# Values' projection of the forgetting attention by seven products, with the roles of stationary and moving operand turned

## The reference

```python
def fox_mixer(h, w_in, b_f, q_gain, k_gain, w_out):
    u = h @ w_in                     # 512 x 1024 times 1024 x (3*1024 + 16)
    q, k, v, f_logit = jnp.split(u, [D_MODEL, 2 * D_MODEL, 3 * D_MODEL], axis=-1)
    q = rms_norm(heads(q), q_gain)
    k = rms_norm(heads(k), k_gain)
    v = heads(v)
    ...                              # causal softmax with a forget term, 16 heads of 64
    return o @ w_out
```

## Time and profile before

| | before |
|---|---|
| time, median of 3 runs | 3028.66 us (3025.91 to 3030.33) |
| span of the profiled execution | 3026.6 us |
| PE busy | 2943.9 us (97%), 17897 matmuls |
| DVE busy | 1770.3 us (58%) |
| ACT busy | 703.9 us (23%) |
| POOL busy | 404.4 us (13%) |
| mean granted TensorE clock | 0.990 |
| HBM traffic | 206.8 MB, mean 68 GB/s |

### The profile page before, as it was taken

One profiled execution on the slowest core, in us unless ns is written; L12 is line 12 of the kernel. 1 busy time (PEld: TensorE's weight loads), 2 busy tenths in 40 slices (PEclk: granted clock), 3 DMA queues, 4 the chain that ended last, 5 costly groups with the idle time before them and its releaser, 6 DMA issues.

```text
span 3026.6 us, 42057 instructions
## 1 busy us (share of the span) xinstructions
PE 2943.9 (97%) x17897; PEld 2496.8 (82%) x17897; DVE 1770.3 (58%) x2388; ACT 703.9 (23%) x1250; POOL 404.4 (13%) x390
## 2 busy tenths in 40 slices
PE   8999999999999999989989999999999999999999
PEld 7878888888778888878678878888888867888888
DVE  4475645564467653531566668887555134888853
ACT  1511100035531110002336532212010174112201
POOL 2112210220002220020023401111020021111101
PEclk9999999999999999999999999999999999999999
DMA  4222221322002223121100022223222200222320
GB/s 137 67 73 91 90 84 60 97 80 73 29 29 84 84 84 112 56 81 47 63 1 4 4 93 84 84 84 105 77 69 84 70 1 28 82 86 84 105 68 37
DMA packets 207573, 209.47 MB, mean 69 GB/s; under 512 B 8996, under 2 KB 206332, under 8 KB 207388
## 3 DMA queue, kind: packets, MB, share of 16 engines
q1 hardware_dynamic: 207100, 206.70, 21.4%
q10 hardware_dynamic: 288, 0.10, 0.0%
HBM read 204.65 MB, written 2.10 MB: 68 GB/s over the span
## 4 chain that ended last, share of the span: by engine, by line
PE 91%; DVE 5%; ACT 2%; issue 1%; POOL 0%; ACTq 0%; DMA 0%; DVEq 0%; POOLq 0%
PE pp L272 63%; PE pp L149 9%; PE pp L1269 4%; PE pp L2881 2%; PE pp L2118 1%; PE pp L1403 1%; PE pp L2101 1%; PE pp L2858 1%; PE pp L1750 1%; DVE arena L348 1%; PE pp L2073 1%; PE pp L2914 1%; PE pp L1426 1%; PE pp L2481 1%; DVE rs L856 1%
## 5 line engine op out<-in xcount | busy, mean ns | idle before, releaser
L272 PE MATMUL pp<-arena 128*128 128x256 f32 (+1 forms) x9072 | 1999.3, 383 | 13.6 <-DVE arena L1091 6.5
L272 PEld LDWEIGHTS pp<-arena 128*128 128x128 f32 x9072 | 1721.6, 190 | 289.9 <-DVE arena L1091 7.7
L149 PE MATMUL pp<-arena 128*128 128x264 f32 (+4 forms) x1312 | 294.4, 384 | 1.2 <-DVE arena L830 1.2
L149 PEld LDWEIGHTS pp<-arena 128*128 128x128 f32 (+3 forms) x1312 | 241.6, 185 | 51.2 <-issue 6.2
L360 ACT COPY arena<-pp 128x528 f32<-128x528 f32 (+1 forms) x62 | 36.1, 582 | 656.3 <-PE pp L272 550.0
L865 POOL TENSOR_TENSOR sq<-sq 128x512 f32<-128x512 f32 (+1 forms) x47 | 78.2, 1664 | 720.8 <-ACT sq L843 717.1
L348 DVE TENSOR_TENSOR arena<-arena 128x256 f32<-128x256 f32 (+5 forms) x196 | 166.0, 870 | 6.5 <-POOL arena L2710 2.4
L2636 ACT ACTIVATE arena<-arena,par 128x528 f32<-128x528 f32 x88 | 68.1, 820 | 385.8 <-DVE arena L2667 385.8
L2710 POOL TENSOR_TENSOR arena<-arena 128x528 f32<-128x528 f32 x44 | 72.0, 1637 | 494.5 <-DVE arena L2679 494.5
L380 DVE TENSOR_TENSOR arena<-arena,pp 128x528 f32<-128x528 f32 (+1 forms) x66 | 46.0, 696 | 140.0 <-PE pp L272 138.0
L321 DVE TENSOR_TENSOR arena<-arena 128x1024 f32<-128x1024 f32 (+2 forms) x66 | 122.9, 1862 | 5.3
(11 more groups left out here) (311 smaller groups left out, 2807.5 us busy)
## 6 DMA issues: line engine op xcount, KB each, us to landing
arena<-in_mlp_w_dram SPq DMA_DIRECT2D x64, 1024.0 KB, 5.5
arena<-in_ffn_up_dram SPq DMA_DIRECT2D x44, 1024.0 KB, 5.1
arena<-in_ffn_down_dram SPq DMA_DIRECT2D x16, 1408.0 KB, 7.3
arena<-in_fox_w_in_dram SPq DMA_DIRECT2D x12, 1024.0 KB, 5.3
arena<-in_lru_w_in_dram SPq DMA_DIRECT2D x8, 1024.0 KB, 7.8
arena<-in_lru_w_out_dram SPq DMA_DIRECT2D x4, 1024.0 KB, 5.2
arena<-in_fox_w_out_dram SPq DMA_DIRECT2D x4, 1024.0 KB, 5.1
arena<-in_rw_wk_dram SPq DMA_DIRECT2D x4, 1024.0 KB, 8.1
```

The lines of the kernel that those rows point to most:

```text
L149: mm = pe.matmul(bank[0:m, h, 0:r.shape[1]], slot[0:kp, kk, j * P:j * P + m], r, start=kt == 0, stop=kt == nk - 1)
L272: return pe.matmul(k.pp[seventh(k, name, n, i) % NB][:, j, 0:hw], stationary[i][:, kk, j * P:(j + 1) * P], moving[i][:, kk, :], start=kk = ...
```

## The change

`fox_va` and `fox_vb` become two seven-product calls, `fox_v0` and `fox_v1`, each over one pair of 256-column blocks, with `turned=True`: the input sums are the stationary operand (128 tokens of them), the weight sums the moving one (256 columns). Products and combination are otherwise those of the other calls. The results go unscaled from DVE into `v` (`v_add`), and ACT scales them there in place, 8 pieces of 128x256 for each call (`v_scaled`), after its `keep_first`. The weight sums get a place of their own (`Sv`, in `raw` and `o`): part 0 of `fox_v0`'s stands inside the combine of `fox_qk3`, part 1 behind `keep_roots`; both parts of `fox_v1`'s stand inside the combine of `fox_v0`, ahead of its add of THREE. POOL copies one input difference (128x1024) into `k.h` after its clears, and PE waits for it ahead of `fox_v0`. The first `values` of attention waits for all 16 scalings. The plan now has 14 tiles here, where it had 8; the number of weight units is the same.

```diff
-def product_seven(pe, k, name, X, S, T, hw, ready, summed):
+def product_seven(pe, k, name, X, S, T, hw, ready, summed, turned=False):
...
         def multiply(i, j, kk):
+            if turned:
+                return pe.matmul(k.pp[seventh(k, name, n, i) % NB][:, j, 0:GW], moving[i][:, kk, j * P:(j + 1) * P],
+                                 stationary[i][:, kk, :], start=kk == 0, stop=kk == half - 1)
...
-    plan_tokens(k, "fox_va", w_in, (2 * D, 2 * D + D // 2), spans, ["act", "dve"])
+    plan_seven(k, "fox_v0", w_in, [(2 * D + GW, 2 * D)])
     k.psum.add(f"fox_sum{NQ - 1}", ["act"] * 4)
-    plan_tokens(k, "fox_vb", w_in, (2 * D + D // 2, 3 * D), spans, ["act", "dve"])
+    plan_seven(k, "fox_v1", w_in, [(2 * D + 3 * GW, 2 * D + 2 * GW)])
...
         turn_roots(e, k, "fox_roots", rspans)
-        product_tokens(e, k, "fox_va", lambda kt, a, b: k.h[:, kt, 1 + a:1 + b], lambda kt: None)
+        e.wait_ge(diff_s, 1)
+        product_seven(e, k, "fox_v0", X, Sv, T, hw, lambda i, kk: None, vsum_s[0], turned=True)
         sums(NQ - 1)
-        product_tokens(e, k, "fox_vb", lambda kt, a, b: k.h[:, kt, 1 + a:1 + b], lambda kt: None)
+        product_seven(e, k, "fox_v1", X, Sv, T, hw, lambda i, kk: None, vsum_s[1], turned=True)
...
         def values(f):
             e.wait_ge(pt_s, 3 * (2 * f + 2))
+            if f == 0:
+                e.wait_ge(v_s, 16)
...
-        read_tokens(k, "fox_va", e, "act", v, k.small[:, 50:55])
+        def v_scaled(n):
+            for q, i in (((0, 0), TWO), ((1, 0), FOUR), ((1, 1), None), ((0, 1), THREE)):
+                if i is None:
+                    e.wait_ge(v_raw, n + 1)
+                else:
+                    was_read(e, k, seventh(k, f"fox_v{n}", 0, i))
+                for t in (2 * q[1], 2 * q[1] + 1):
+                    part = v[:, t, v_col(n, q):v_col(n, q) + GW]
+                    e.activation(part, part, ACT.Copy, scale=k.small[:, 50 + t:51 + t]).then_inc(v_s, 1)
+
+        was_read(e, k, seventh(k, f"fox_qk{NQ - 1}", 0, THREE))
+        keep_first(e, k, "fox_v0", 0, tq, hw)
+        v_scaled(0)
         roots(NQ - 1)
-        read_tokens(k, "fox_vb", e, "act", v[:, :, D // 2:D], k.small[:, 50:55])
+        was_read(e, k, seventh(k, "fox_v0", 0, THREE))
+        keep_first(e, k, "fox_v1", 0, tq, hw)
+        v_scaled(1)
...
+        def v_add(n):
+            def add(e, quarter, w, y, op, g):
+                t, c = 2 * quarter[1], v_col(n, quarter)
+                ins = e.tensor_tensor(v[:, t:t + 2, c:c + GW], w, y, op)
+                if g is None:
+                    ins.then_inc(v_raw, 1)
+                else:
+                    freed(k, g, ins)
+            return add
...
         keep_roots(e, k, "fox_roots", rspans)
-        was_read(e, k, k.psum.base["fox_roots"])
-        read_tokens(k, "fox_va", e, "dve", v, k.small[:, 50:55])
+        e.wait_ge(qk_s, 2 * KT)
+        weight_sums(e, k, "fox_v0", 0, Sv, vsum_s[0], 1)
+
+        def next_v(part):
+            def f(e):
+                filled(e, k, seventh(k, "fox_v0", 0, THREE if part else SIX))
+                weight_sums(e, k, "fox_v1", 0, Sv, vsum_s[1], part)
+            return f
+
+        combine(e, k, "fox_v0", 0, tq, uq, hw, v_add(0), middle=next_v(0), late=next_v(1))
         normed(NQ - 1)
-
-        read_tokens(k, "fox_vb", e, "dve", v[:, :, D // 2:D], k.small[:, 50:55])
+        combine(e, k, "fox_v1", 0, tq, uq, hw, v_add(1))
...
+        filled(e, k, k.psum.base["fox_f"])
+        qin_s.wait(e, 1)
+        e.tensor_copy(in_place(X, T, 0, KH, hw), Tq[3]).then_inc(diff_s, 1)
```

More of the change, by code:

```diff
@@ L1348, in stage_fox @@
     Sq = [k.work(at_v + i * KH * GW, KH, GW) for i in range(3)]
+    Sv = [raw[:, 0:2, :].rearrange("p a b -> p (a b)").rearrange("p (t n) -> p t n", t=KH),
+          o[:, 0:2, :].rearrange("p a b -> p (a b)").rearrange("p (t n) -> p t n", t=KH),
+          raw[:, 2:4, :].rearrange("p a b -> p (a b)").rearrange("p (t n) -> p t n", t=KH)]
     Tq = T + [k.work(at_v + 3 * KH * GW, KH, hw)]
@@ L1351, in stage_fox, with v_col @@
     qsum_s, qin_s = [weight_steps(k, 1) for n in range(NQ)], input_steps(k, 4)
+    vsum_s = [weight_steps(k, 1) for n in range(2)]
+    v_raw, v_s, diff_s = (k.sem("fox_" + n) for n in ("v_added", "v_scaled", "difference_kept"))
+    def v_col(n, quarter):
+        return (2 * n + (0 if quarter[0] else 1)) * GW
     osum_s, oin_s = weight_steps(k, 2), input_steps(k, 4)
@@ L1544, in raw_add @@
             return add
+        def v_add(n):
[7 more added lines that the diff above has]
+            return add
         def next_weights(n, part):
             def f(e):
-                filled(e, k, seventh(k, f"fox_qk{n}", 0, THREE if part else SIX))
-                weight_sums(e, k, f"fox_qk{n + 1}", 0, Sq, qsum_s[n + 1], part)
-            return f if n + 1 < NQ else None
+                if n + 1 < NQ:
+                    filled(e, k, seventh(k, f"fox_qk{n}", 0, THREE if part else SIX))
+                    weight_sums(e, k, f"fox_qk{n + 1}", 0, Sq, qsum_s[n + 1], part)
+                elif part == 0:
+                    weight_sums(e, k, "fox_v0", 0, Sv, vsum_s[0], 0)
+            return f
         def normed(n):
```

## The result

| | before | changed |
|---|---|---|
| time, median | 3028.21 us (3025.91 to 3030.33, 4 runs) | 3039.76 us (3036.83 to 3041.07, 4 runs) |
| ratio, 95% interval | | 1.0037 [1.0025, 1.0048] |
| span of the profiled execution | 3026.6 us | 3039.3 us |
| PE busy | 2943.9 us, 17897 matmuls | 2946.0 us, 17865 matmuls |
| mean granted clock | 0.990 | 0.987 |

The forecast was 7.3 slower, 3036.0 us, with a range of 3031.5 to 3039.5: the first median lies 0.3 us above the range, the second one (3037.07) inside.

A forecast was written before the change was run, and what follows sets the result against it. PE was taken as the bound, 91% of the span. Terms -6.7 + 3.9 + 6.9 - 0.2 + 4.2 - 0.8 gave +7.3 us, 3036.0 from the median 3028.66, range 3031.5 to 3039.5.

The forecast's parts named there:

- the clock: Behind the two new idle stretches around v0 and v1, matmuls run at 1.2 GHz: +4.2 us, bounds 3.0 and 5.9.
- rivals 2 and 4: 2: stalls come, clock holds, +3.1, 3031.8, chance 0.11; 4: one of two clock falls missed, +5.2, 3033.9, chance 0.10.
- Matmuls, -6.7: On PE, fox_va and fox_vb (55.50 us) give way to two calls of 24.41 us: -6.7 us.
- Start of v0, +3.9: Ahead of v0, PE takes ONE and TWO at once, so waits for the next logarithm too: +3.9 us.
- Inside v0, nothing: SIX's weight sums from DVE are ready 0.4 us early, and THREE's delayed add is covered too: nothing.
- Between v0 and v1, +6.9: Sums wait 0.9 us for THREE's add; v1 idles 6.0 for ACT, whose scalings precede the roots: +6.9 us.
- End of v1, -0.2: At v1's end, the last add is one instruction of 0.69 us where two took 0.88: -0.2 us.
- fox_out, -0.8: Six more tiles make start_early true, so fox_out's 0.89 us wait for the last output copy goes: -0.8 us.
- POOL's copy, nothing: POOL's copy behind its clears takes 0.9 to 2.3 us, needed by PE 100 us later: nothing.
- tiles free in time (1): Both calls start where the sums end, without idle stretches or lower clock: -6.8 us, 3021.9; chance 0.07.
- rival 3: Clock falls at every gap, a third at the wait for THREE, each 3.0 us: +12.1, 3040.8; chance 0.10.

The follow-up runs named there:

- the second set: The changed kernel, unaltered, run again seven times beside other kernels: median 3037.07 us against 3028.63 before, ratio 1.0027.
- the dummies' run: Changed kernel plus 9 dummy matmuls in each of fox_v0 and fox_v1 between taking ONE's tile and TWO's: 3030.61 us, ratio 1.0006 of before.
- ONE before TWO: Changed kernel with fox_v0 and fox_v1 running all of ONE before taking TWO's tile: 3032.71 us, ratio 1.0012 of the kernel before.
- the pairs: ACT's roots as two logarithms, then two exponentials: on the moved-weight-sums version 3017.50 us (0.9963), again 3018.62 (0.9966); on the kernel before, plain values, 3023.41 (0.9985).
- the moved weight sums: Changed kernel with ONE before TWO, v0's scaling behind roots(3), and both calls' part 1 weight sums moved: 3021.54 us, ratio 0.9978 of before.
- the one with `fox_out` held back: Changed kernel with start_early forced false, so fox_out doesn't start early: run once, 3038.91 us.
- the one with ACT's scaling moved: Changed kernel with ACT's scaling of v0 moved behind roots(3) and the copy of v1's ONE: 3032.21 us, ratio 1.0013 of before.

## Why the prediction was right

The mechanism came as forecast, term by term, and one term was too small: the clock, 4.2 us where 5.9 were lost. That put the traced cost at the upper bound of the sum (6.1 to 9.0 us without its extra half microsecond) and the first median just outside the range. How near the number came has some luck in it as well. The first set's executions were all of the slower kind, with the lower mean clock; three of the seven in the second set, at 3032.4 to 3034.4 us, lie near rivals 2 and 4 instead.

*Matmuls, -6.7.* Right. At full clock the turned calls are 24.39 us, as the dummies' run shows, and the others 24.41.

*Start of v0, +3.9.* Right in place and size: the wait is 5.73 us instead of 1.79, on the third logarithm.

*Inside v0, nothing.* Right for the changed kernel; SIX has no wait. That the cover was thin was shown when PE started earlier: 2.31 us of wait (the prediction named 0.4 us of cover).

*Between v0 and v1, +6.9.* Measured 0.92 + 5.84 = 6.8. The scalings took 0.91 us a pair in SBUF where I took 0.81 from reads out of PSUM.

*End of v1, -0.2, and fox_out, -0.8.* Measured 1.16 against 1.28 of idle, and 0.89 gone.

*Clock, +4.2.* The mechanism was right and the size too small: 27.43 + 27.25 - 2 x 24.41 = 5.9 us, at the upper bound of 5.9. The mean of four rows drew in two shorter stretches (1.5 and 1.7), where both new gaps were as costly as the dearest row; the second set of runs gave 27.35 and 27.21, so it is no chance of one execution, though three of eleven may have escaped it, as said above. The dummies, which leave PE no long idle stretch ahead of the calls, turn the loss off. The Trainium skill (TensorE: Matmul & The Clock Gate, What's actually happening) puts the ramp's penalty under 1% of a typical span and advises against fitting a count of slow matmuls. 5.9 us are 0.2% of this span and agree with that; but of a change worth some 10 us they are more than half, so that leaving them out would have given rival 2's 3031.8. The Trainium skill also has idle leading to the lower level there, and these traces agree: 0.50 behind both long waits.

*POOL's copy, nothing.* Right. It took 1.03 us beside two DVE adds that read PSUM and kept their 0.68 and 0.69, and the idle behind them kept its 1.60 us. The timeline of POOL:

```profile
623.69 1.03 POOL L1682 COPY arena<-arena 128x1024 f32<-128x1024 f32 x1
```

and of DVE beside it:

```profile
623.22 0.68 DVE L380 TENSOR_TENSOR arena<-sq,pp 128x512 f32<-128x512 f32 x1
623.93 0.69 DVE L383 TENSOR_TENSOR arena<-arena,pp 128x512 f32<-128x512 f32 x1
...
626.94 0.69 DVE L1565 TENSOR_TENSOR arena<-arena,pp 128x512 f32<-128x512 f32 x1 [1.60 <-PE pp L275]
```

Summed up, the part between `fox_qk3` and `fox_out` is 9.1 us by the trace (10.04 to the scores, 0.9 back at `fox_out`) where 7.3 were forecast; the clock's 1.7 is nearly the whole difference. The medians say 11.5 and 8.4, and 9.1 lies inside both intervals (1.0025 to 1.0048 and 1.0015 to 1.0038, that is 7.6 to 14.5 and 4.5 to 11.5 us). What the first set has above 9.1 is not explained: it can be scatter of the clock, or the early 2.1 us. One thing in the frame was loose. I took 3026.6 us for the profiled execution's time, but that is its span, and a listed time is 1.8 us more than the span of the same execution (3041.07 and 3039.3 in the changed kernel). So most of the 2.1 us between span and median was no difference between executions; the sum is not touched by it.

The rivals: tiles free in time (1) is what the remedies made nearly true, and rival 3 had the price of a fall right but not a third fall. Rivals 2 and 4 (the clock holds at both stalls, or at one) happened in no trace of the changed kernel; the three quicker executions of the second set have times near theirs and were not traced, so for them it is open.

## What to carry to other kernels

Fewer matmuls bring their time only if the next PSUM tiles are free when PE gets there: write the order of tiles out, find for each new tile the one that lay there before, and ask when its reader is done. A call that takes two tiles before its first matmul waits for the second reader, and a slow reader (here one with a table load for each instruction) then costs its full pace; running the tiles one behind the other cured most of that wait and laid bare the next one, SIX's for the weight sums. Put work that nobody waits for, such as a scaling in place, behind the reads that free tiles, and add the lower clock to the price of an idle stretch of some microseconds that you make on TensorE: here up to 3.0 us each.

Before you trust a difference of a few microseconds between medians, look at the mean clock of each execution and compare a distance inside the trace: here one kernel's two traces differed by 8.6 us, and by 0.01 us over the stretch that the change touches.

## What the hardware showed that I had not expected

The lower clock comes behind short waits too, and not always. The pattern of sums, 0.9 us of wait, one more sum, 1.9 us of wait stood ahead of v1 in two kernels: behind it the matmuls ran at 1.00 in the one with the dummies and at 0.50 for 6 us in the one with ONE before TWO (27.36 us). The first had worked on dummies in the gap ahead of v0, the second had waited 2.31 us inside v0; whether that decides, these runs don't show. Stretches of that kernel, PE alone:

```profile
758.00:759.00 1.00, 0.00 (x0) 0.58 0.00 0
759.00:765.00 6.00, 5.98 (x14) 0.50 0.00 0
```

Likewise the waits of 1.64 and 0.31 us ahead of `fox_qk2` and `fox_qk3` are the same in the nine traces without the pairs (before, changed, and the runs up to the moved weight sums). In seven of them `fox_qk2` took 26.0 to 26.1 us and `fox_qk3` 24.41, in one it was the other way round, in one both took 24.41. In the three runs with pairs, where the 0.31 is gone, all six calls took 24.34. Among the nine, that is up to 1.7 us from run to run which no edit of the values explains.

A wait of 5.7 to 5.8 us ahead of v0 or v1 brought the lower clock all seven times that one was traced (two each in the changed kernel, its second run and the one with `fox_out` held back, one in the one with ACT's scaling moved), for 2.8 to 3.0 us of loss each. Nine useless matmuls in each such gap gave 5.9 us back over the two calls.
